# Expert rows beside the second token tile: VectorE and ScalarE one group later, 40 groups instead of 60, TensorE sums the rest

## The reference

```python
def reference(x, ...):
    x = first_block(x, c, ...)        # adaLN, four mixers with gates, MLP of width 4096, final norm
    return second_block(x, ...)       # attention, then peer_ffn, then a norm

def peer_ffn(xn, w_peer_q, sub_keys, expert_u, expert_v):
    qh = (xt @ w_peer_q).reshape(T, 8, 2, 128)
    s = einsum('thpd,hpnd->thpn', qh, sub_keys)          # 8 heads, 2 halves, 128 keys
    sv, si = top_k(s, 16)
    cand = sv[:, :, 0, :, None] + sv[:, :, 1, None, :]   # 16 x 16 candidates
    best, pick = top_k(cand.reshape(T, 8, 256), 16)      # 16 experts of 16384 a head
    gates = softmax(best)
    hval = einsum('cd,chkd->chk', xc, expert_u[idx])
    return einsum('chk,chkd->cd', gates * gelu(hval), expert_v[idx])
```

## Time and profile before

| | before |
|---|---|
| time, median of 3 runs | 1630.73 us (1630.6 to 1633.61) |
| the profiled execution's own time | 1623.74 us |
| its span, first to last instruction | 1622.4 us |
| TensorE busy | 1206.0 us (74%) |
| VectorE busy | 995.7 us (61%) |
| ScalarE busy | 410.3 us (25%) |
| GpSimd busy | 464.6 us (29%) |
| moved by DMA | 512.60 MB, mean 316 GB/s |
| mean granted TensorE clock | 0.885 |

### The profile page before, as it was taken

The page is one execution under the profiler, slowest core; times in us unless marked ns, Lnnn a source line. Parts: engine busy times, 40 slices in busy tenths (PEclk is TensorE's granted clock), DMA queues, the critical chain, the costliest instruction groups (busy, mean ns, idle before and its releaser), DMA issues.

```text
span 1622.4 us, 13984 instructions
## 1 busy us (share of the span) xinstructions
PE 1206.0 (74%) x4802; PEld 750.1 (46%) x4802; DVE 995.7 (61%) x2041; ACT 410.3 (25%) x1025; POOL 464.6 (29%) x333
## 2 busy tenths in 40 slices
PE   2986987589979988878567776649775666756675
PEld 2864554256658447544244553545335422222222
DVE  6187887611112115765767455877746999888764
ACT  2142111210012211333221111332422243333322
POOL 0014455300000001222223342332322556554540
PEclk9998997789989998979878998777897889899988
DMA  9522554458866575978979999897997999999996
GB/s 376 225 111 98 226 214 188 180 196 331 339 224 244 196 267 196 397 306 316 356 289 415 406 419 425 331 393 313 374 425 290 376 418 422 421 421 421 421 422 249
DMA packets 58247, 512.60 MB, mean 316 GB/s; under 512 B 6720, under 2 KB 9024, under 8 KB 10304
## 3 DMA queue, kind: packets, MB, share of 16 engines
q0 software_dynamic: 36864, 268.45, 40.8%
q1 hardware_dynamic: 20160, 239.67, 37.6%
q10 hardware_dynamic: 1152, 3.59, 0.6%
HBM read 510.63 MB, written 1.05 MB: 315 GB/s over the span
## 4 chain that ended last, share of the span: by engine, by line
PE 37%; DMA 23%; DVE 15%; issue 3%; ACT 3%; DVEq 0%; SPq 0%; ACTq 0%
PE ps L519 16%; PE ps L915 7%; PE ps L859 7%; DMA arena<-in_euv,arena 6%; DMA ring<-in_w 6%; DMA ring<-in_euv,arena 4%; DVE arena L1777 4%; DVE xr L1801 4%; PE ps L606 3%; DMA K<-in_euv,arena 2%; PE ps L1042 2%; DVE ring L1777 1%; DMA ring<-in_qkv 1%; DMA ring<-in_wout 1%; DMA ring<-in_bb 1%
## 5 line engine op out<-in xcount | busy, mean ns | idle before, releaser
L2342 POOL DMA_INDIRECT arena<-in_euv,arena x166 | 235.9, 1421 | 653.3 <-DVE arena L1771 320.7
L519 PE MATMUL ps<-arena,ring 128*128 128x128 f32 (+1 forms) x2320 | 315.1, 300 | 30.5 <-DMA ring<-in_qkv 6.4
L519 PEld LDWEIGHTS ps<-arena,ring 128*128 128x128 f32 x2320 | 302.4, 203 | 50.1 <-issue 10.1
L1777 DVE CUSTOM_DVE_ANT_0 arena<-arena 128x1024 f32<-128x1024 f32 x166 | 201.1, 1221 | 29.1 <-DMA arena<-in_euv,arena 27.9
L1042 PE MATMUL ps<-arena 128*128 128x512 f32 x240 | 132.2, 695 | 75.8 <-ACT arena L2226 75.8
L859 PE MATMUL ps<-ring,arena 128*128 128x512 f32 x320 | 152.7, 631 | 15.6 <-DVE arena L1134 6.5
L1801 DVE SCALAR_TENSOR_TENSOR xr<-arena,xr 128x1024 f32<-128x1024 f32 x106 | 135.9, 1282 | 39.6 <-ACT arena L2238 34.1
L519 PE MATMUL ps<-arena 128*128 128x128 f32 (+4 forms) x684 | 122.7, 331 | 44.3 <-ACT arena L1867 22.3
L2342 POOL DMA_INDIRECT ring<-in_euv,arena x76 | 98.8, 1300 | 194.6 <-DVE xr L1801 152.2
L915 PE MATMUL ps<-ring,arena 128*128 128x512 f32 x256 | 127.1, 656 | 35.4 <-DMA ring<-in_w 35.4
L519 PEld LDWEIGHTS ps<-arena 128*128 128x128 f32 (+1 forms) x684 | 101.7, 209 | 71.5 <-issue 48.0
(11 more groups left out here) (300 smaller groups left out, 1299.3 us busy)
## 6 DMA issues: line engine op xcount, KB each, us to landing
ring<-in_w SPq DMA_DIRECT2D x32, 2048.0 KB, 10.5
ring<-in_gates SPq DMA_DIRECT2D x16, 2048.0 KB, 8.3
ring<-in_ada SPq DMA_DIRECT2D x12, 2048.0 KB, 8.5
ring<-in_qkv SPq DMA_DIRECT2D x12, 2048.0 KB, 9.1
ring<-in_g SPq DMA_DIRECT2D x8, 2048.0 KB, 8.0
ring<-in_pq SPq DMA_DIRECT2D x8, 2048.0 KB, 8.4
ring<-in_wp SPq DMA_DIRECT2D x5, 2048.0 KB, 7.5
ring<-in_w_o SPq DMA_DIRECT2D x4, 2048.0 KB, 7.8
```

The costliest lines, as they stand in the source:

```text
L519: ins = te.matmul(o, l, r, start=(i == 0), stop=(i == len(pairs) - 1))
L1777: ins = v.tensor_tensor_reduce(out=x, in0=x, in1=xn[:, tt, :], scale=1.0, scalar=0.0, op0=ALU.mult, op1=ALU.add, accum_out=hv[:, n % 16:n ...
L2342: gp.indirect_dma_start(slots[i], None, A["euv"], bass.IndirectOffsetOnAxis(ap=idx[:, n // 16 % 4, e % 16:e % 16 + 1].bitcast(U32), axis=0 ...
```

## The change

- `AMONG` goes from 60 to 40 and `JOIN` from 60 to 44. The 7 last slots join at pick 90 instead of 130.
- `on_vector(n)` is true for `n < 2 * AMONG` alone, so VectorE adds picks 0 to 79 and TensorE all 176 later ones. Before, VectorE added 0 to 119 and every fourth after.
- A new generator `behind` wraps `last_order` for VectorE and ScalarE: it holds the units of tile 1 back until the next group is yielded. TensorE and GpSimd go by the old order.
- The four `normalize` calls of a softmax move from the units `pt` to a unit `norm` of their own, one unit after `soft`. This holds for both tiles.
- The PSUM banks are divided differently: tile 1's MLP has four "main" banks and two "misc"; the second block of both tiles has three and five, before two and six.
- VectorE waits for `shares` of seven groups ago before a dot whose pick TensorE adds, since nothing else keeps the dot results from being overwritten.
- The flag `scored` is delayed by one group, so that `choose` of tile 1 stands behind the units that it reads.

```diff
-    yield from (proj(3, 1), proj(4, 0), pt(0, 0), proj(4, 1), pt(0, 1), pv(0, 0), proj(5, 0), pt(0, 2), pv(0, 1),
+    yield from (proj(3, 1), (("norm", 0), 1), proj(4, 0), pt(0, 0), proj(4, 1), pt(0, 1), pv(0, 0), proj(5, 0), pt(0, 2), pv(0, 1),
...
-    yield from (gate(0, 1), gate(1, 0), gate(1, 1), (("branch", 0, 0), 2), pt(1, 0), (("branch", 0, 1), 2), pt(1, 1),
+    yield from (gate(0, 1), (("norm", 1), 1), gate(1, 0), gate(1, 1), (("branch", 0, 0), 2), pt(1, 0), (("branch", 0, 1), 2), pt(1, 1),
...
-AMONG = 60
-
-JOIN = 60
+AMONG = 40
+
+JOIN = 44
...
+def behind():
+    held = []
+    for u, tt in last_order():
+        if tt and u != ("finish",):
+            held.append((u, tt))
+            continue
+        yield u, tt
+        if u[0] == "group":
+            yield from held
+            held = []
...
 def on_vector(n):
-    return n < 2 * AMONG or n % 4 == 0
+    return n < 2 * AMONG
...
-                    pools.update({"main": (0, 1), "misc": (2, 3, 4, 5)})
+                    pools.update({"main": (0, 1, 2, 3), "misc": (4, 5)} if tt else {"main": (0, 1), "misc": (2, 3, 4, 5)})
...
-                    pools.update({"misc": (2, 3, 4, 5, 6, 7)})
+                    pools.update({"main": (0, 1, 2), "misc": (3, 4, 5, 6, 7)})
...
-                elif what == "pt":
-                    normalize(i, tt, half)
+                elif what == "norm":
+                    for c in range(4):
+                        normalize(i, tt, c)
...
+                if not on_vector(GROUP * g):
+                    v.wait_ge(sig("shares"), g - 7)
...
-            for u, tt in last_order():
+            for u, tt in behind():
```

More of the change, by code:

```diff
@@ L191, in last_order @@
     total, cost, g = sum(c for _, c in units), 0, 0
-    due, scored = [], False
+    due, scored = [], [False, False]
     def group(g):
@@ L198, in group @@
         weigh = None
-        if due and (due[0][0] < 8 or scored) and (k % 2 == 0 or len(due) > 4 - k // 2):
+        if due and (due[0][0] < 8 or scored[0]) and (k % 2 == 0 or len(due) > 4 - k // 2):
             s, q = due.pop(0)
@@ L203, in group @@
         yield ("group", g), None
+        scored[0] = scored[1]
         if weigh is not None:
@@ L208, in last_order @@
         yield u, 1
-        scored = scored or u == ("pq", 0)
+        scored[1] = scored[1] or u == ("pq", 0)
         cost += c
@@ L1815, in finish @@
                 v.wait_ge(sig("row_added"), sum(not on_vector(n) for n in range(128 * tt + 128)))
-                v.wait_ge(*added[tt])
+                if tt in added:
+                    v.wait_ge(*added[tt])
                 v.wait_ge(sig("l_g"), 16)
```

## The result

| | before | after |
|---|---|---|
| median of 6 runs | 1628.9 us (1626.76 to 1633.61) | 1643.02 us (1640.55 to 1650.39) |
| profiled execution | 1623.74 us | 1650.39 us |
| its span | 1622.4 us | 1648.8 us |
| TensorE busy | 1206.0 us | 1305.7 us |
| VectorE busy | 995.7 us | 912.7 us |

The ratio is 1.009, 95% interval 1.0064 to 1.0116: **slower by 0.9%**, where I had forecast 3.5 us faster. Part of it is tile 0, which ends at 661.4 us here and at 654.5 in before; with the same work there, the profiles of this study have it anywhere from 654 to 661.

The account below looks back on a forecast made before the run. The prediction took DMA to bound the tail and tile 1's MLP, and waits between engines the other stretches. Tail +82.5 us and savings of 86 us moved the median 1630.7 by -3.5 to 1627 us, range 1603 to 1656.

Parts of the forecast that it names:

- the sum 82.5 - 86: Whole kernel: tail 82.5 us longer against 86 us saved in tile 1's stretches and tile 0, net -3.5 us.
- A: Tile 1's gates, recurrence, merges and output: 10 picks fewer at 1.33 us each, 13 us shorter, bounds 5 and 20.
- B: Tile 1's MLP, DMA share 1.00: 12 picks fewer at near 2.49 us each, 29 us shorter.
- C: Tile 1's attention and branches: 13 picks fewer at 1.33 us, plus `norm` and smaller gains, 29 us shorter.
- D: Tile 1's output product, norm and queries: 5 picks fewer and shorter waits, 12 us shorter, bounds 7 and 15.
- tile 0: The first tile, without gathers: `normalize` goes ahead of its waits, 3 us shorter, bounds 0 and 5.
- Tail, forecast +82.5: After the last `pq`: 166 gathers left at 2.49 us plus some 4 us, 417 us; bounds 75 and 90 longer.
- The rival "slower": Tile 1: picks leave stretches that were not full, saving only 56 us; 1657 us, chance 0.24.
- Costed at nothing: Lag, PSUM banks, `JOIN`, the added wait for `shares` and TensorE's extra sums were each given no cost or gain.
- Its deciding point: Tile 1's length, 619.5 us before: if over 537 us after the change, the kernel is slower.
- TensorE bounds the tail: Tail: full groups of sums take 5.38 us against 4.98 of DMA, 35 us on top; 1662 us, chance 0.06.

Follow-up runs that it names:

- e2: The kernel before with only the number changed, AMONG 40 and JOIN 44: 1660.58 us.
- e5: The changed kernel without the units `norm`, so that `pt` normalizes its own pair again, which also shifts the planner's groups: 1651.17 us.
- e7: The changed kernel with the planner's cost of the MLP's units at 0, so only 2 of the 40 groups fall there: 1660.47 us.
- e3: The changed kernel without the lag, VectorE and ScalarE going by the old order of units: 1651.23 us.
- e9: The changed kernel with ScalarE not holding back its `pt` and `pv` copies: 1638.71 us.
- e4: The changed kernel with every fourth later pick added by VectorE again: 1644.42 us.
- e1: The changed kernel with the old number, AMONG 60 and JOIN 60: 1610.98 us.
- e11: The changed kernel with 63 groups, JOIN 60 and the MLP's units at planner cost 5 instead of 7: 1617.29 us.

## Why the prediction was wrong, by its own steps

**The step that failed is the worth of a group in tile 1 against its worth in the tail**, the sum 82.5 - 86. The profiles have +88.5 in the tail and -69.5 in tile 1, where 83 of the 86 were to come. A and B missed by 22.3 us each in opposite directions, so that their sum, forecast 42, measured 42.0: luck, since neither price was right. What is left of the miss is C (7.7), D (5.8), tile 0 (3) and the tail (6). Its parts:

- *Tail, forecast +82.5.* Measured +88.5, near the upper bound of 90. That exactly 90 gathers would be out was right, and 2.49 us a pick and 421 GB/s too (423 / 166 = 2.55 with the ends). What I gave too little is the gap, 4 us for what measured 9.7 (423 - 413.3): with 90 allowed and all landed early, the 8 us around the last `pq` moved 116 GB/s. The rows had it: in before 130 gathers were left, 323.7 us, in a tail of 334.5, a gap of 10.8.
- *B, forecast -29 as if paced by DMA.* -6.7 in after, -22.7 in e2. The share of 1.00 in the earlier trace rows said that it was full; it did not say that the time would follow the bytes. The share, which was to stay at 0.98 or more, fell to 0.89. TensorE was idle 34.8 us for weight loads in before's B, and these waits only fell to 26.0 (22.3 in e2), with loads that landed in 11.3 us against 12.0. The other difference between e2 and after is the wait before the norm at B's end, 8.68 against 16.34 (15.34 in before), from where the planner put a group (e5), and 4.7 us of TensorE's busy time. The rival "slower" had this mechanism (the two-buffer ring stays late), with 18 us. The Trainium skill ("DMA: Bandwidth & Descriptors", section "SWDGE vs HWDGE vs iDMA") has each DMA engine take turns between the two kinds of queues; that a load's landing hardly fell with a third fewer gathers, and that its waits nearly went in e7 with hardly any, agrees.
- *A, forecast -13, borrowed from C.* -35.3 (-24.8 by the number alone), 2.5 us a pick in e2 and not 1.33. 14.0 of the 35.3 are TensorE's busy time, 130.8 to 116.8 us for the same matmuls at a clock of 0.85 and then 0.96, which I had costed in C only. A + B is 318.8 in e2 and 316 to 329 in after and in e3 to e7, against 366.3 before, so the two may share a limit; no run shows one.
- *C, forecast -29.* -21.3. The number alone gives 9.3 (0.8 a pick, not 1.33), and the clock's part was 2.5 us of busy time, where 0.41 a pick made 5.3. TensorE's waits for `normalize` in C went from 20.5 to 2.5 us and those for weight loads from 13.6 to 6.2. The first and longest fell by 12.7 us as forecast (2.51, within "2 to 3 us"), but half of it came back as 6.11 behind ScalarE's copy, the lag's own doing, shown by e9.
- *D, forecast -12.* -6.2, and -7.4 in e2.
- *Tile 0, forecast -3.* Not seen: its end lay between 654 and 661 us in profiles of the same work.
- *Costed at nothing.* `JOIN` and the added wait: right. VectorE's picks to TensorE: right, since full sum groups took 3.70 us (below), not 5.38. Lag and banks: wrong, 8.2 and 9.8 us undone alone, both gains.

Sorted by part of the change instead of by stretch: the number was forecast at +82.5 - 68 = +14.5 us (all of the 86 but 8, 2 and 5 for the units' order and 3 of tile 0) and measured +30; all else was forecast at -18 and measured at -17.5. The second sum came out right by luck, since lag and banks were to give nothing. The first is the miss: 6 us in the tail, 4 in tile 1, and the rest in tile 0 (6.2 later in e2's profile) and in what executions differ by.

**The rivals.** "Slower: the picks leave stretches that were not full" had the right direction, at 1643 and not 1657. Its deciding point, tile 1 over 537 us, held: 550.0. Its reason held in C only: A, with a share of 0.84, gave 2.5 us a pick, the tail's full price, and A and B together saved 42.0 us in after and 47.5 in e2, where it gave 27. "TensorE bounds the tail" is refuted by TensorE's timeline of after, where the sums of a full group, eight records, take 3.7 us with idle behind them:

```profile
1405.18 3.70 PE L1057 MATMUL ps<-arena 128*128 128x512 f32 x8 [0.84 <-ACT arena L2246]
...
1415.14 3.71 PE L1057 MATMUL ps<-arena 128*128 128x512 f32 x8 [1.28 <-ACT arena L2246]
1420.80 3.71 PE L1057 MATMUL ps<-arena 128*128 128x512 f32 x8 [1.96 <-ACT arena L2246]
```

The step there was right: 0.46 us a record at the 2.4 GHz level. Of the rows of eight behind a wait in this view of the tail, 32 took 3.70 or 3.71 us, two 5.40 and one 6.53 (the chain above shows one of 5.42); the 32 stand behind 0.2 to 2.0 us of idle time, the three behind 2.25 and 3.29; yet two rows of sixteen behind 2.6 and 2.8 us took 7.13, the fast pace, so the idle time alone doesn't tell them apart. The granted clock of the tail is 0.96. The Trainium skill ("TensorE: Matmul & The Clock Gate", section "HAM oscillation — how this bites in real kernels") tells its rule of a kernel that waits longer than this for each transfer between its bursts. My reading, that every short burst would start at the low clock, went beyond it: here bursts of 3.7 us with 1 to 2 us between them stand at the high level.

**The chances.** The slower case had 0.24 from its rival and 0.39 in all. It deserved more: before's own tail put the gap at 10.8 us and the tail's price at the bound of 90, and that alone takes the sum above nothing.

## What to carry to other kernels

Work moved from places where it is partly hidden into a stretch paced by one resource costs its full price there (here 5 us a group), and what it frees must be measured per unit, since the saving falls as more is taken (3.1 us a group, then 1.1). A DMA share of 1.00 over a stretch with two kinds of queues doesn't say that the stretch is as long as its bytes: ask which transfer the engines wait for, and whether it would start earlier. When several edits come together, run the number alone and the structure alone first: here two runs split +14 into +30 and -17. And where a planner places work by the costs of units, adding a unit moves that work too; print the list before and after, or an experiment on one part changes two.

## What was not expected of the hardware

- TensorE's sums in the tail ran at 0.96 of the full clock when they were denser (329 us busy of 422.6) and at 0.88 when a quarter of them was left out (284 of 421, e4): with more work the mean clock was higher, and the time of the tail did not change. The other tails go the same way: 0.89 in e2 (286 of 423), 0.95 in e1 (257 of 328.5).
- GpSimd's record of one indirect gather is 0.94 us in some rows and 1.5 to 1.98 in others with the same shape; it did not bound anything here, and what the second value depends on was not tried.
- A weight load of 2 MB landed in 11.3 us beside 25 gathers in 177 us, hardly below the 12.0 beside 37 in 184; without gathers it was 7.8.
- Still open: half of what the lag saves, why TensorE's clock in A is higher with the new banks, why A costs nothing up to 11 groups and so much behind them, and what else e11 lost in A.
